# Down projection by seven quarter products instead of plain matmuls, in two parts between the blocks of gate and up

## The reference, cut to what matters

```python
D_FF = -(-8 * D_MODEL // (3 * 256)) * 256          # 2816 = 22 blocks of 128

hn = rmsnorm_2(h, ffn_norm_w[i])
gate, up = jnp.split(hn @ w_gate_up[i], 2, axis=-1)
h = h + (jax.nn.silu(gate) * up) @ w_down[i]
ple_gate = jax.nn.sigmoid(rmsnorm_2(h, ple_norm_w[i]) @ w_ple_gate[i])
h = h + ple_gate * (p[i] @ w_ple_proj[i])
```

## Time and profile before

| | |
|---|---|
| three runs, median (lowest to highest) | 1189.83 us (1189.13 to 1191.66) |
| the profiled execution: own time | 1191.32 us |
| the profiled execution: span, first to last instruction | 1189.5 us |
| mean granted TensorE clock | 0.996 |
| gate and up on TensorE | 789 to 1012 us |
| down on TensorE | 1012 to 1132 us |

### The profile page before, as it was taken

The page is one execution under the profiler, slowest core; times in us unless marked ns, Lnnn a source line. Parts: engine busy times, 40 slices in busy tenths (PEclk is TensorE's granted clock), DMA queues, the critical chain, the costliest instruction groups (busy, mean ns, idle before and its releaser), DMA issues.

```text
span 1189.5 us, 17906 instructions
## 1 busy us (share of the span) xinstructions
PE 1167.8 (98%) x7362; PEld 985.2 (83%) x7362; DVE 757.3 (64%) x1197; ACT 554.4 (47%) x886; POOL 97.3 (8%) x114
## 2 busy tenths in 40 slices
PE   7999999999999999999999989999999999999997
PEld 5887778788777887887777788889999999888886
DVE  6786555555567765548887785596767676444455
ACT  5425444536625445214547445465555555322254
POOL 0191011111000100100000200000000000100000
PEclk9899999999999999999999999999999999999999
DMA  9763279999721433992112101136655555633321
GB/s 375 290 205 113 67 261 313 243 271 327 180 71 54 133 111 117 336 244 67 54 59 84 36 4 37 48 113 215 219 181 183 179 194 173 239 98 98 102 87 73
DMA packets 57792, 185.97 MB, mean 156 GB/s; under 512 B 6544, under 2 KB 6672, under 8 KB 52592
## 3 DMA queue, kind: packets, MB, share of 16 engines
q1 hardware_dynamic: 47088, 127.29, 32.1%
q0 software_dynamic: 9776, 56.10, 17.3%
q10 hardware_dynamic: 848, 1.45, 0.3%
HBM read 178.52 MB, written 52.43 MB: 194 GB/s over the span
## 4 chain that ended last, share of the span: by engine, by line
PE 89%; DVE 4%; ACT 3%; issue 1%; DMA 1%; POOL 0%; ACTq 0%; DVEq 0%
PE pb L752 86%; PE pb L1015 1%; PE pb L843 1%; DMA aR<-a_spill 1%; DVE wlo L2059 1%; ACT Y L1501 1%; DVE xqs L2062 0%; DVE xT L2059 0%; DVE xlo L2059 0%; PE pb L1176 0%; ACT xhi L1501 0%; DVE tmpf L2059 0%; DVE ssq L2059 0%; ACT xq L1501 0%; ACT outT L1501 0%
## 5 line engine op out<-in xcount | busy, mean ns | idle before, releaser
L2059 DVE TENSOR_TENSOR wlo<-raw,whi 128x1024 fp32r<-128x1024 f32 (+1 forms) x210 | 254.8, 1215 | 112.9 <-ACT whi L1501 112.0
L752 PE MATMUL pb<-hhi,wlo 128*128 128x512 f32 (+2 forms) x696 | 271.1, 389 | 2.6 <-DVE wlo L2059 2.6
L752 PE MATMUL pb<-hhi,whi 128*128 128x512 f32 (+2 forms) x696 | 270.3, 388 | 0.0
L752 PE MATMUL pb<-hlo,whi 128*128 128x512 f32 (+2 forms) x696 | 269.0, 395 | 0.7 <-DVE tmpf L2059 0.7
L1501 ACT ACTIVATE whi<-raw 128x1024 fp32r<-128x1024 f32 (+1 forms) x210 | 214.6, 1037 | 84.1 <-DMA raw<-w_all 66.0
L752 PE MATMUL pb<-xlo,whi 128*128 128x256 f32 x616 | 174.9, 284 | 0.5 <-DVE xlo L2059 0.4
L752 PE MATMUL pb<-xhi,wlo 128*128 128x256 f32 x616 | 174.3, 283 | 0.0
L752 PE MATMUL pb<-xhi,whi 128*128 128x256 f32 x616 | 174.3, 283 | 0.0
L752 PEld LDWEIGHTS pb<-hlo,whi 128*128 128x128 f32 (+1 forms) x696 | 130.9, 188 | 30.6 <-issue 3.3
L752 PEld LDWEIGHTS pb<-hhi,wlo 128*128 128x128 f32 (+1 forms) x696 | 131.0, 188 | 30.3 <-DVE wlo L2059 3.5
L752 PEld LDWEIGHTS pb<-hhi,whi 128*128 128x128 f32 (+1 forms) x696 | 130.7, 188 | 27.3
(11 more groups left out here) (417 smaller groups left out, 1873.0 us busy)
## 6 DMA issues: line engine op xcount, KB each, us to landing
raw<-w_all SPq DMA_DIRECT2D x121, 512.0 KB, 4.2
w_sums<-w_all POOLq DMA_DIRECT2D x30, 1024.0 KB, 13.6
raw<-w_sums SPq DMA_DIRECT2D x88, 256.0 KB, 2.9
raw<-w_all SPq DMA_DIRECT2D x66, 256.0 KB, 3.1
w_sums<-w_sums POOLq DMA_DIRECT2D x10, 1024.0 KB, 11.0
adab<-ada_d SPq DMA_DIRECT2D x12, 512.0 KB, 11.8
gbt<-ada_d SPq DMA_DIRECT2D x12, 512.0 KB, 7.4
raw<-w_all SPq DMA_DIRECT2D x13, 384.0 KB, 3.1
```

The lines of the kernel that those rows point to most:

```text
L752: return e.matmul(out, lhs, rhs, start=start, stop=stop, skip_group_check=True)
L2059: return e.tensor_tensor(out, a, b, op)
```

## The change

Down is computed by seven quarter products too. An output pair of blocks (rows 2v and 2v+1) is a unit "d" v, beside the units "g" u of gate and up. Its input halves are the even and the odd blocks u, so a product over the first ten blocks has 5 blocks of 3 matmuls of 128 x 256, and one over the last twelve has 6. The list `UNITS` sets the order: 10 units g, four units d over the first ten blocks (n = 10 to 13), 12 units g, four units d over the last twelve (n = 26 to 29). A unit n is counted over this list; at the first unit of a block of units (`LEADS`) the products of the last unit are finished first, and the order of the next ones differs. The activation is kept as combinations: an even u stores 2 (the block's first half of tokens, and the sum of both halves), an odd u stores 5, after three more DVE instructions behind its `finish`. There is one buffer for the gate (`gbuf`) and one each for even and odd units (`ev`, `od`). The spill is gone, and the last two units' activations lie over the input combinations (`aX`), so their `act_high` waits for the last product of gate and up. POOL also builds sums of the down weights: the steps into `w_sums` all come ahead of the loads of `xT` now, and 24 DMAs into `w_sums_down` stand where 12 stood. The weight sums and quarters of down are chunks of one product each (640 or 768 columns). `high`, `square`, `gained` and `squared` of output rows move between the products of the last four units.

```diff
+UNITS = [("g", u) for u in range(10)] + [("d", v) for v in range(4)]
+UNITS += [("g", u) for u in range(10, FFB)] + [("d", v) for v in range(4, 8)]
+LEADS = (0, 10, 26)
+NG = 25
+DEPTH = {n: 4 if kind == "g" else 5 if i < 4 else 6 for n, (kind, i) in enumerate(UNITS)}
 def products():
+    for n in range(len(UNITS)):
+        if n in LEADS:
+            out += [(7, n - 1), (3, n - 1), (4, n - 1)] if n else []
+            out += [(1, n), (5, n), (1, n + 1), (5, n + 1), (6, n), (2, n), (7, n), (6, n + 1), (3, n), (2, n + 1), (4, n)]
+        elif n - 1 not in LEADS:
+            out += [(1, n), (7, n - 1), (5, n), (3, n - 1), (6, n), (4, n - 1), (2, n)]
...
+def packed(order):
+        if out and len(out[-1]) == 1 and DEPTH[k[1]] == DEPTH[out[-1][0][1]] == 4:
+            out[-1].append(k)
...
-            for j in range(4):
-                G.wait_ge(*LO(("a", j)))
-                e.dma_start(spill[j], act_slot(j)).then_inc(SPILL.sem, 16)
...
+            sum_step(sumd[0], down[0], False, RUND)
+            sum_step(sumd[1], down[0], False, RUND)
+            sum_step(sumd[0], down[1], True, RUND)
...
+            for k in range(DEPTH[n]):
+                T.wait_ge(*right_key(n, k, x))
+                rh, rl = right(n, k, x)
+                t = mm3(PB[b][:, 0:256], hi[:, 4 * h + k, :], lo[:, 4 * h + k, :], rh, rl, k == 0 and p_ in (1, 5), k == DEPTH[n] - 1)
...
             def act_high(n):
+                    A.wait_ge(*FV_(("y", n)))
+                    if n == NG - 1:
+                        A.wait_ge(*PROD((4, NG)))
+                    copy(act_slot(u)[0], od[:, 1:6, :] if u % 2 else ev[:, 0:2, :]).then_inc(HI.sem, 1)
...
+            def finish(n):
+                if kind == "d":
+                    tt(rows[:, 256:512], rows[:, 256:512], rsb[:, 256:512], ALU.mult)
+                    V.wait_ge(*PROD((4, n)))
+                    stt(rows[:, 0:256], last, -1.0, rsb[:, 0:256], ALU.mult, ALU.mult).then_inc(FV_.sem, 1)
+                    V.wait_ge(*FV_(("a", n)))
+                    update(n, 1, rows)
...
+                if u % 2:
+                    tt(od[:, 2:4, :], od[:, 0:2, :], ev[:, 0:3:2, :], ALU.subtract)
+                    stt(od[:, 4, :], od[:, 0, :], -1.0, od[:, 1, :], ALU.mult, ALU.subtract)
+                    stt(od[:, 5, :], ev[:, 0, :], -1.0, od[:, 1, :], ALU.mult, ALU.subtract).then_inc(FV_.sem, 1)
+                else:
+                    tt(ev[:, 1, :], ev[:, 0, :], ev[:, 2, :], ALU.add).then_inc(FV_.sem, 1)
```

On DVE, at the first unit of a block of units, and at the end:

```diff
+                    late(n - 1)
+                    conv_for(4, n - 1, LOOK + 1)
+                    gate_late(n - 1)
+                    if n < NG:
+                        act_low(n - 2)
+                    finish(n - 1)
+                    if n > NG:
+                        act_low(n - 2)
...
+            late(29)
+            gate_late(29)
+            conv("st", len(PACKS) - 1)
+            normed(5)
+            finish(29)
+            normed(6)
+            normed(7)
```

More of the change, by code:

```diff
@@ L685, in pool_program, with sum_step @@
             done = [0]
-            def sum_step(out, src, add):
-                for c in range(0, RUN, 2048):
+            def sum_step(out, src, add, run=RUN):
+                for c in range(0, run, 2048):
                     n = done[0]
@@ L700, in pool_program @@
             whole = [w_all[QOFF + q * 128 * RUN:QOFF + (q + 1) * 128 * RUN] for q in range(4)]
+            DOFF = QOFF + 512 * RUN
+            down = [w_all[DOFF + q * 128 * RUND:DOFF + (q + 1) * 128 * RUND] for q in range(4)]
             sum_step(sums[0], whole[0], False)
@@ L2006, in scalar_program @@
+            conv("st", len(PACKS) - 1)
+            high("d", 6, V_PN)
+            square("d", 6)
+            high("d", 7, V_PN)
+            square("d", 7)
             conv("pg", 0)
@@ L2686, in vector_program, with updated, update @@
             square_sum(6)
[L2688 to L2694 removed]
+            def updated(n, i):
+                return FV_(("r", n, i)) if n < NG else TXR(("d", 2 * UNITS[n][1] - 8 + i))
+            def update(n, i, src):
+                m = 2 * (UNITS[n][1] % 4) + i
+                V.wait_ge(*(TXR(("w", m)) if n < NG else updated(n - 16, i)))
+                tt(xT[:, m, :], xT[:, m, :], src, ALU.add).then_inc((FV_ if n < NG else TXR).sem, 1)
@@ L2736, in vector_program, with act_low, conv_for, normed @@
+            def act_low(n):
+                kind, u = UNITS[n]
+                if kind == "g":
+                    hi, lo = act_slot(u)
+                    low(("a", u), lo, od[:, 1:6, :] if u % 2 else ev[:, 0:2, :], hi)
+            def conv_for(p_, n, look=LOOK):
+                conv("st", AT[p_, n][0], look)
+            def normed(m):
+                gained("d", m, V_PN)
+                squared("d", m)
             third_seed(0)
@@ L2931, in weights @@
                 out.append(blocks_of(a["w_gate_up_2"][0], slice(128 * (FFB * half + u), 128 * (FFB * half + u + 1)), k0, 4))
+    for half in range(2):
+        for odd in range(2):
+            for first, last in ((0, 10), (10, FFB)):
+                for v in range(4):
+                    c = slice(128 * (2 * v + half), 128 * (2 * v + half) + 128)
+                    out.append(blocks_of(down[first + odd:last:2].reshape(-1, D), c))
     return np.concatenate(out)
```

445 lines of the change are left out of this document (251 added, 194 removed).

## The result

The change makes the kernel slower: 1204.61 us, the median of four runs (1202.93 to 1205.45), against 1190.51 (1189.13 to 1191.66) for the kernel before on the same chip; the ratio is 1.0117, with a 95% interval of 1.0100 to 1.0135. The prediction was 1195.1 (1190.8 to 1199.0): the side is right, the size is not, 14 us lost where 5 were counted. The profiled execution took 1205.45 us.

What follows compares the result with a forecast made beforehand. TensorE's work was taken to bound the kernel. The terms -9.4 + 4.2 + 0.6 + 2.6 + 3.9 + 2.3 + 1.1 = +5.3 on a median of 1189.83 gave 1195.1 us, range 1190.8 to 1199.0.

Steps and rivals of the forecast that it cites:

- matmuls: In down, 924 narrow matmuls at 0.12 us replace 528 wide ones taking 120.33 us: a gain of 9.4 us.
- five odd units, second block: Gate and up: chunk behind each odd unit's copy delayed 2.04 us against 1.27 to spare; 0.85 each, +4.2 us.
- first hand-over: Gate and up to down: the last odd unit's low part on DVE delays the chunk for (5,11); +0.6 us.
- second hand-over, the wait: Start of down's second part: (1,26) waits for the low part of u = 20; +2.6 us.
- last four units: End of down: `high` and `square` stand ahead of weight chunks on ACT, so TensorE waits; +3.9 us.
- last product, the wait: End of down: the chunk for (4,29) stands behind `gate_late(29)` on DVE; +2.3 us.
- last rival: All matmuls at the skill's pace: a loss of 6 us, not a gain of 9.4; 1210.5 or more; chance 0.01.
- a ring whose cover I had called thin: Three-slot load ring: loads take 3.1 us, are late at more than 3.7; costed at nothing.
- Restarts: After each of 11 larger TensorE waits, about 0.1 us more is lost, bounds 0 and 0.2; +1.1 us.
- faster rival: ACT and DVE conversion runs further ahead, hiding waits: 1180.4 us, or 1188.1 at half of all waits; chance 0.10.
- the cancelling one: Three fixed-order waits stay, 9.1 us and 0.7 of restarts, the others hidden: 1190.2, no change; chance 0.16.
- thin waits: First hand-over and last four units, 4.5 us, and their restarts: 1190.1 if they vanish, 1199.6 if they double.

Runs made afterwards that it cites:

- six moves: The five moves, plus the chunk of (5,28) converted ahead of the first unit's norm work on ACT and DVE: 1184.26 us, 0.9940 of the kernel before.
- those of three: Changed kernel with chunks ahead of every gate and up copy, u = 20 ahead of silu and `finish(25)`, last chunk alone ahead of `gate_late(29)`: 1189.65 us, ratio 0.9977.
- five moves: Those of three, plus (5,n+1)'s chunk ahead of the last odd unit's copies at both hand-overs, and norm work behind chunks: 1183.72 us, 0.9931 of the kernel before.
- filled waits: Changed kernel with 19 and 16 matmuls that nobody reads put into TensorE's two longest waits: 1201.30 us, 1.0082 of the kernel before.

## Why the prediction was wrong in size

| step of the prediction | counted, with restart | lost in the trace after | |
|---|---|---|---|
| matmuls | -9.4 | -9.6 | right |
| five odd units, second block | 4.7 | 4.6 | right |
| first block of gate and up | 0 | 2.2 | missed |
| first hand-over | 0.7 | 3.2 | too small |
| way back to gate and up | 0 | 0.6 | missed, a load |
| second hand-over, the wait | 2.7 | 2.8 | right |
| last four units | 4.2 | 4.7 | right |
| last product, the wait | 2.4 | 2.4 | right |
| half clock after two waits | in "0 to 0.2" | 3.0 | missed |
| ahead of gate and up | 0 | 0.3 | |
| sum (of unrounded rows) | 5.3 | 14.1 | |

The matmul row is what the others leave of the 14.1 us of span. Its check is the kernel of six moves, which keeps all of the change's matmuls and few of its waits: a stretch of 335.2 us against 343.9, so 8.7 less with 0.9 lost in it. The changed kernel and those of three and of five moves give the same 334.3 us of stretch once what each lost is taken off. Narrow matmuls stand 0.12 us apart in down as well. My last rival is out with that, the pace that the Trainium skill gives in "TensorE: Matmul & The Clock Gate", section "Back-to-back issue gap": by the estimate worked out from it in the prediction (81 ns or more for a narrow matmul, 131 for a wide one), no order could have beaten the kernel before, and the six moves do.

**The step that failed first** is the one from the second block to the first, in the sentences "Together 2.04 us against 1.27" and "In the first block odd units have the other pairing: there the chunk behind the copy is due 1.44 us later, and nothing waits. Even units add 0.33 us only."

The sum of 2.04 us was right: it is what the trace after shows between `finish` and the chunk, in both blocks. The room was wrong. For the first block I took the 1.27 us of another place and added the 1.44 us by which the chunk is due later, 2.71 in all. The trace of before has 1.58 at that place, as `finish` stands behind one more chunk on DVE there and comes later itself; no row of the prediction shows that place. So the odd unit's chunk is late by 0.08 us, with no delay from the unit before.

The even units' part of it is that I let each unit start from nothing: 1.05 us of the odd unit's delay reach the even unit, through `wlo`, `gate_late` and a low part of 1280 columns, and its 1.27 us of room aren't enough; out of the last pair the delay reaches the hand-over. Together that is 2.2 + 2.5 = 4.7 us of the miss. The run with the chunk ahead of every copy shows it: the first block loses nothing, and the hand-over's remaining wait measures 0.62 us, which is the 0.6 that I had counted for it.

The 0.6 us of the way back are not shown to be of this kind; there a load was late, in a ring whose cover I had called thin and costed at nothing.

**The second** is "Restarts. ... the bounds are 0 and 0.2". A restart costs 0.26 us, made of 0.15 before the first matmul and 0.11 behind it (0.93 for a wait of 0.67), of which 0.1 was in my five waits; that part was off by little. But the two longest waits bring the clock to half, 1.5 us each: 3.0 us that no row of before could show, since TensorE never waited over 0.4 us there behind 790 us. The filled waits show that idleness is the cause.

4.7, 3.0 and 0.6 are 8.3 of the 8.8 us between the forecast of +5.3 and +14.1; the rest is tenths in other rows.

**Right:** the five waits (0.66 instead of 0.85, each 21 us from the next), 2.54 us for `aX` where I had 2.6, 2.11 for the last chunk where I had 2.3, and 0.70, 1.02, 0.33 and 1.02 in the last units. It is partly luck that these rows agree so well: each wait was counted up to 0.4 us too long and each restart 0.16 too short. The norm work's place did cost what I said. That sum steps hurt nobody was nearly right: loads took twice as long there, and TensorE waited 0.63 us at 534.55 in this execution and 0.5 in one of the others, in the rest not at all; I had said it would not wait. The 10.4 us of the earlier trace rows are mostly of loads of 512 KB, whose usual time is 4.2, so 2.5 times the usual and not three. In the faster rival, half of all waits makes 1187.8 and not 1188.1; nothing hangs on it. Of the rivals, the cancelling one and the faster one assumed hidden waits; none was hidden. The range failed because its upper end doubled only the thin waits, and no case let a delay outlive its unit or the clock fall.

## What to carry to other kernels

When an instruction ahead of a chunk grows in a queue that is written in fixed order, read the room at each place from its own rows, as the same chunk may have less of it there (1.58 us where 2.71 were reckoned here), and follow the delay through the next two or three units, not to the first wait that it causes: here it arrived where the pattern changes. Price a wait of TensorE by the distance of matmul starts, and one like those of over 2 us here with a half clock behind it. Where the engines have room on average (here 68% and 49%) and the waits are of order, moving a dozen lines may turn a loss of 1.2% into a gain of 0.7%: the scheme was sound, and its schedule was what was measured.

## What the runs showed of the hardware

- TensorE's clock fell to half after 10 of 13 waits of 2.1 to 2.5 us in the profiled executions of this change and its variants, and after none of the waits of up to 1.6 us behind 790 us. It falls within 1.4 us after TensorE has gone on, and costs 1.2 to 1.6 us each time (2.7 in one). What decides between falling and not falling for the same wait stays open.
- A wait that the profile gives as 0.67 us costs 0.93, and a stall too short to be listed as a wait still costs 0.2 to 0.4 us; seven of these made 2.2 us in a stretch where the view of waits is empty.
- Loads beside accumulating DRAM to DRAM steps took 9.9 us instead of 4.2 (512 KB, medians of 17); TensorE waited beside them once, 0.63 us, in this execution.
